# The first attention's value projection in two blocks side by side, its index weights in four, with a PSUM bank of their own

## The chip, the core and the metric

The kernel runs on one NeuronCore of a Trainium2 chip. The metric is the device time of one launch in microseconds (us), as the median of three runs; the kernel before takes 1764.91 us (1761.79 to 1765.24). The core has a matrix engine (TensorE, "PE" in the rows; its weight loads are listed apart as "PEld"), a vector engine (DVE), a scalar engine (ACT), GpSimd (POOL), and SyncE (SP), which issues most of the DMAs. Each works through its own list of instructions in order and waits for the others at semaphores.

## The reference

Two model blocks follow each other over 1024 tokens of width 1024. The first normalises its input, scales and shifts it by a vector made from a condition, projects it (`w_in`), and sends the parts through a state space mixer and through an attention in which each query keeps the 256 best keys by an index score. The second is a block with dilated window attention and a chunked scan. What the change touches is the projection of the first attention's values `v` (64 wide) and of the index weights `wi` (8 wide):

```python
h = rms_norm(x, norm_g) * (1 + scale[:, None]) + shift[:, None]
proj = h @ w_in
xa, za, q, k, v, zb, qi, ki, wi, ga, gb = jnp.split(proj, IN_SPLITS, axis=-1)
...
s = jax.nn.relu(jnp.einsum('bqhd,bkd->bqhk', qib.astype(f32), k_idx32)) * IDX_SCALE
score = jnp.einsum('bqh,bqhk->bqk', wb.astype(f32), s)
_, sel = lax.top_k(score, top_k)
```

Here `qib`, `k_idx32` and `wb` are `qi`, `ki` and `wi`; 64 + 8 = 72 output features are at stake.

## The kernel before

The projections are a list of *units* (`unit_plan`, L230). A unit fills one PSUM bank with an output of 128 features by 512 tokens: PE multiplies in eight steps `k`, one for each 128 input features, accumulating in the bank; then ACT copies the bank out (`evac`, L1957) and counts `s_free`. `unit_bank` (L322) says which bank a unit has, and a unit waits until the last unit of its bank is copied out.

The first ten units (`FIRST_ORDER`) work in fp32 on `h_whole`, the transposed, normalised input. Of these `("small", 0)` and `("small", 1)` (units 0 and 4 of the list) make `v` and `wi` together, with 72 weight columns, for the first and the second half of the tokens: eight matmuls each, 72 output rows by 512 tokens. In the trace one fp32 matmul is two weight loads and two matmul records; in this kernel these two units therefore are 16 + 16 records of "128*72 128x512 f32" at L1416. `("small", 2)` and `("small", 3)` make the keys and index keys with full 128 columns. `("small", 4)` and `("small", 5)` transpose what units 0 and 4 left in `vwT` (L1367), and wait for the copying out of unit 4.

The order on PE is written out by hand (L1652 to L1679): ten warming products (L1653); the transposes of the input's first half (L1626); the products for scale and shift (`mod_products`, L1639, whose weights are loaded by four DMAs, and `mod_turned`, L1647); steps 0 to 3 of unit 0 (`unit(0, 0)`); the other scale and shift products; steps 0 to 3 of unit 1; steps 4 to 7 of unit 0 and of unit 1; unit 2; the transposes of the second half; unit 3; units 4 to 9. Each step `k` of unit 0 waits until DVE (even `k`) or ACT (odd `k`) has scaled and shifted its part of `h_whole`. The transposes of the input use banks 2 to 7 in the first half and banks 4 to 7 in the second (`input_bank`). After unit 9 the index scores (L1694) begin, in banks 2 to 7.

ACT works in this order around the place: squares of the input for the norm, scaling of half of `h_whole` (L2147), more squares, an `Exp`, the copying out of units 0 and 1, some `Exp` and `Sin` for the state space part, the eight scaled copies of the second half's transposes (L2177), then units 2, 3, 4 and so on. `evac` of unit 0 or 4 is one instruction of 72 partitions by 512 (L1964).

A fact of the listing that is needed later: a row such as "128*64 128x128 f32" says that the matmul uses 128 rows and 64 columns of the array (a *form* of the array, here called the 64-column form) and moves 128x128 elements through it. Other stages of this kernel use narrow forms already: L1445, L1860 and L1865 (64 columns), L1716 (32 columns), L1393 (16 columns), L1526 (64 rows by 32 columns).

Of the kernel before, what the change touches and what calls it, by code (L numbers as in the profile page):

```python
# [10 lines left out]
ACT = mybir.ActivationFunctionType  # L11
AX_X = mybir.AxisListType.X

P = 128
# [199 lines left out]


SMALL_COLS = 216


NORM_PARTS = ((0, 2), (2, 4), (4, 8))
# [102 lines left out]
def unit_bank(u):  # L322
    if UNITS[u][0] in ("gb1", "gate0", "gate1"):
        return 0
    if UNITS[u][0] in ("q", "zs0", "zs1") or UNITS[u] in LATER_ORDER:
        return u % 2
    if UNITS[u][0] == "xa":
        return UNITS[u][1] % WIDE_BANKS
    if UNITS[u][0] == "pair0":
        return UNITS[u][1] % 2  # L330
    if UNITS[u][0][:3] == "woA":
        return OUT_BANKS[(u - FIRST["woA0"]) % len(OUT_BANKS)]
    return (u + 2) % WIDE_BANKS
# [13 lines left out]
def layer_kernel(nc, x, mods, first_weights, loads, groups, params, consts, rows, alibi, out, x2_dram, gates_dram, q_dram,  # L347
                 sums_dram, res_dram):
    ctx = ExitStack()
    with ctx:  # L350
# [933 lines left out]
        def _(pe):  # L1284
            mm = nc.tensor.matmul

            def operands(name, i):

                whole = name in WHOLE
                w = W[:, LOADS.index(name) % 2, :] if name in LOADS else None

                def weights(steps, k, c0, n):
                    if name == "small":
                        return small_w[:, k, c0:c0 + n]
                    if name in PLANAR:
                        return planes(chunks(MADE_AT[name][k], 1))
                    if steps == KD and name in MADE_AT:
                        v = chunks(MADE_AT[name][k], 1)[:, c0:c0 + n]  # L1300
                        return v if whole else parts(v)
                    v = w.rearrange("p (k n) -> p k n", k=steps)[:, k, c0:c0 + n]
                    return v if whole else parts(v)

                def acts(tile, k, t0, n):
                    if whole:
                        return h_whole[k][:, t0:t0 + n]
                    return h_parts(k, t0, n) if tile is hT else parts(tile[:, k, t0:t0 + n])

                half = (i % 2) * 512  # L1310
                full = slice(0, 512)
                if name[:4] == "gate":
                    return 1, [(full, lambda k: ones, lambda k: gate[:, 512 * int(name[4]):512 * int(name[4]) + 512])]
                if name == "small" and i < 2:
                    return KD, [(full, lambda k: weights(KD, k, P, 72), lambda k: acts(hT, k, half, 512))]
                if name == "small":
                    return KD, [(full, lambda k: weights(KD, k, 0, P), lambda k: acts(hT, k, half, 512))]
                if name == "qi" and i % 2 == 0:
                    return KD, [(slice(TOPK, 512), lambda k: weights(KD, k, (i // 2) * P, P),
                                 lambda k: acts(hT, k, TOPK, 512 - TOPK))]  # L1320
                if name == "glu":
                    c0 = (i % 2) * 512 + (i // 4) * P
                    h0 = ((i // 2) % 2) * 512
                    return 4, [(full, lambda k: weights(4, k, c0, P), lambda k: planes(yaT[:, k, :])[:, h0:h0 + 512, :])]
                if name == "ao":
                    return 4, [(full, lambda k: weights(4, k, (i // 2) * P, P), lambda k: planes(zaT[:, k, half:half + 512]))]
                if name == "bo":
                    h0 = (i // 8) * 512
                    return 4, [(full, lambda k: weights(4, k, (i % 8) * P, P), lambda k: block_planes(ybT[:, k, h0:h0 + 512]))]
                if name in ("out0", "out1"):  # L1330
                    src = mT
                    return KD, [(full, lambda k: acts(src, k, i * P, P), lambda k: weights(KD, k, 0, 512))]
                if name[:4] == "pair":
                    what, h = PAIR_UNITS[i]
                    c0 = P * "qkvz".index(what)
                    return KD, [(full, lambda k: weights(KD, k, c0, P), lambda k: acts(hT, k, h * 512, 512))]
                if name[:2] == "wo":
                    src = mixS if name[2] == "S" else mixA
                    return KD, [(full, lambda k: acts(src, k, i * P, P), lambda k: weights(KD, k, 0, 512))]

                return KD, [(full, lambda k: weights(KD, k, (i // 2) * P, P), lambda k: acts(hT, k, half, 512))]

            def unit(u, share=None):
# [43 lines left out]
                if name == "dt":  # L1387
# [7 lines left out]
                                          stop=(k == KD - 1 and (a, b) == PRODUCTS[-1]), skip_group_check=True)  # L1395
                    last.then_inc(s_unit, 1)
                    return
                rows_ = slice(0, 72 if name == "small" and i < 2 else P)
                steps, pieces = operands(name, i)
                some = range(steps)  # L1400
                if share is not None and len(pieces) == 1:
# [4 lines left out]
                for (cols, lhs, rhs), span in spans:  # L1406

                    for k in span:
                        if (name, i) == ("small", 0):
                            pe.wait_ge(s_hta if k % 2 else s_htv, k // 2 + 1)  # L1410
                        if (name, i) == ("xbc0", 1):
                            pe.wait_ge(s_hlow, KD + KD + k + 1)
                        left, right = lhs(k), rhs(k)
                        o = ps[rows_, unit_bank(u), cols]
                        if whole:
                            last = mm(o, left, right, start=(k == 0), stop=(k == steps - 1))  # L1416
                            continue
                        if len(right.shape) == 4:
                            o = o.rearrange("p (b t) -> p b t", t=P)
                        for a, b in PRODUCTS:  # L1420
                            moving = right[:, :, b] if len(right.shape) == 3 else right[:, :, :, b]
                            last = mm(o, left[:, :, a], moving, start=(k == 0 and (a, b) == PRODUCTS[0]),  # L1422
                                      stop=(k == steps - 1 and (a, b) == PRODUCTS[-1]))
# [192 lines left out]
            def turn_input(n):  # L1616

                k, half = turned(n)
                if k == 0:
                    pe.wait_ge(s_xn, 4 * half + 4)  # L1620
                if 6 <= n < KD:
                    pe.wait_ge(s_xt_read, n - 5)
                elif n >= KD:
                    pe.wait_ge(s_xt_read, max(n - 3, KD))
                for j in range(4):
                    last = nc.tensor.transpose(ps[:, input_bank(n), j * P:(j + 1) * P],  # L1626
                                               XR0[:, 4 * half + j, k * P:(k + 1) * P], ident)
                last.then_inc(s_xt, 1)
# [319 lines left out]
        def _(act):  # L1948
# [8 lines left out]
            def evac(u):  # L1957
# [3 lines left out]
                bank = ps[:, unit_bank(u), :]  # L1961
                half = slice((i % 2) * 512, (i % 2) * 512 + 512)
                if name == "small" and i < 2:
                    last = A(vwT[0:72, half], bank[0:72], ACT.Copy)  # L1964
                elif name == "small" and i < 4:

                    for tile, rows_ in ((kT1, slice(0, 64)), (kiT, slice(64, 128))):
# [1341 lines left out]
```

## Time and profile before

| | |
|---|---|
| median of three runs | 1764.91 us (1761.79 to 1765.24) |
| profiled execution, its time | 1763.56 us |
| profiled execution, span from first to last instruction | 1761.8 us |
| PE busy | 1724.0 us, 98% of the span |
| PE's waits over 0.1 us, before 81 us | eight, 6.4 us together; of it 0.17 us after 38 us |
| DVE, POOL, ACT busy | 67%, 50%, 46% |

In a row of the timeline the first number is the start in us from the span's start, the second the length, then engine, line, operation, what is written and read, the form, and how many records were merged; in brackets the idle time just before and what ended it. A matmul's record begins when its data start to move and lasts longer than its place in the stream: records of one engine overlap, so the price of a matmul in a dense stream is the distance between starts. A weight load can overlap the matmul before it. The table of waits and the groups say who waits for whom; the rows themselves stand below.

### The profile page before, as it was taken

The numbers are of one execution on the slowest core, as the hardware profiler recorded it, in microseconds if no ns is written. First come the engines' busy times: TensorE is split into PE (matmuls) and PEld (weight loads), VectorE is DVE, ScalarE is ACT, GpSimd is POOL, SyncE is SP. The second block draws the span as 40 slices with busy tenths as digits, with TensorE's granted clock in tenths as the row PEclk, the third lists the DMA queues.
The fourth block names the chain that finished last, engine by engine and source line by source line (L and its number), as shares of the span: only waits on it lengthen the run. The fifth ranks groups of instructions, "written<-read, shape, count | busy, mean of one in ns | idle before, by whom it ended". The sixth has DMA issues, their size and how long they took to land.

```text
span 1761.8 us, 30529 instructions
## 1 busy us (share of the span) xinstructions
PE 1724.0 (98%) x11938; PEld 891.6 (51%) x11938; DVE 1182.8 (67%) x2237; ACT 813.6 (46%) x1628; POOL 887.1 (50%) x805
## 2 busy tenths in 40 slices
PE   8999999999999999999999999999999999999998
PEld 5534455555444466544544455544455555555543
DVE  5759889999999788532345677966155565654637
ACT  4523554443322577412332468733255555555710
POOL 0511443652671222696911177969556555772750
PEclk9999999999999999999999999999999999999999
DMA  9010111102321112212512346512211111111512
GB/s 396 32 54 36 55 49 62 71 37 102 161 96 48 73 67 103 120 48 96 201 63 94 111 145 198 186 54 96 68 40 53 56 42 51 35 52 55 216 58 96
DMA packets 53375, 161.87 MB, mean 92 GB/s; under 512 B 7056, under 2 KB 21776, under 8 KB 49008
## 3 DMA queue, kind: packets, MB, share of 16 engines
q1 hardware_dynamic: 49008, 136.36, 21.8%
q0 software_dynamic: 4224, 23.56, 3.4%
q8 instruction: 95, 1.56, 0.4%
q14 instruction: 48, 0.39, 0.1%
HBM read 129.35 MB, written 27.39 MB: 89 GB/s over the span
## 4 chain that ended last, share of the span: by engine, by line
PE 67%; DVE 20%; ACT 4%; POOL 3%; DMA 3%; issue 2%; SPq 0%; DVEq 0%; ACTq 0%; POOLq 0%
PE ps L1422 28%; PE ps L1901 15%; DVE small L2684 6%; PE ps L1416 4%; DVE arena L2437 4%; PE ps L1762 2%; PE ps L1445 2%; PE ps L1486 2%; PE ps L1544 2%; PE ps L1920 2%; DMA hT<-in_mods 2%; PE ps L1518 1%; PE ps L1694 1%; PE ps L1459 1%; PE ps L1526 1%
## 5 line engine op out<-in xcount | busy, mean ns | idle before, releaser
L1422 PE MATMUL ps<-hT,W 128*128 128x512 bf16 x2424 | 536.5, 380 | 4.1 <-ACT arena L2004 3.2
L1422 PEld LDWEIGHTS ps<-hT,W 128*128 128x128 bf16 x2424 | 235.7, 98 | 288.3 <-issue 10.2
L989 POOL TENSOR_TENSOR W<-W 128x512 bf16<-128x512 f32 x133 | 153.9, 1193 | 248.5 <-DMA W<-in_loads 181.8
L1422 PE MATMUL ps<-W,arena 128*128 128x512 bf16 x936 | 208.2, 380 | 0.0
L2111 ACT ACTIVATE arena<-arena,small 128x128 f32<-128x128 f32 (+9 forms) x192 | 123.1, 642 | 139.0 <-DVE small L2514 119.6
L1422 PEld LDWEIGHTS ps<-W,arena 128*128 128x128 bf16 x936 | 91.2, 97 | 112.0
L2684 DVE TENSOR_SCALAR_CACHE_REDUCE small<-arena,small 128x640 bf16<-128x640 f32 (+1 forms) x124 | 126.5, 1077 | 1.1
L974 POOL TENSOR_TENSOR arena<-arena 128x512 f32<-128x512 f32 (+1 forms) x62 | 104.8, 1690 | 43.9 <-DMA arena<-gates_scratch 20.1
L1422 PE MATMUL ps<-arena,W 128*128 128x512 bf16 x576 | 125.0, 379 | 0.6 <-POOL arena L1050 0.6
L2120 ACT ACTIVATE arena<-arena,small 128x128 f32<-128x128 f32 (+9 forms) x192 | 113.9, 644 | 18.6 <-DVE small L2472 18.6
L1901 PE MATMUL ps<-arena,W 128*128 128x512 bf16 x492 | 112.9, 379 | 0.0
L2490 DVE TENSOR_TENSOR arena<-ps,arena 128x384 bf16<-128x384 f32 (+2 forms) x128 | 57.0, 466 | 64.4 <-ACT arena L2088 41.1
L3148 DVE TENSOR_TENSOR arena<-ps,arena 128x512 f32<-128x512 f32 x70 | 50.9, 728 | 63.3 <-PE ps L1901 63.3
L1422 PEld LDWEIGHTS ps<-arena,W 128*128 128x128 bf16 x576 | 56.2, 98 | 69.4 <-POOL arena L1050 1.1
L1901 PE MATMUL ps<-hT,W 128*128 128x512 bf16 x384 | 88.4, 380 | 0.0
L2437 DVE TENSOR_TENSOR arena<-arena,small 128x512 f32<-128x512 f32 (+2 forms) x74 | 82.7, 1143 | 0.7
L2009 ACT ACTIVATE arena<-ps 128x512 f32<-128x512 f32 x48 | 28.3, 596 | 118.5 <-PE ps L1422 70.5
L1109 POOL COPY arena<-small 128x128 bf16<-128x128 bf16 x32 | 17.2, 538 | 130.3 <-DVE small L2437 130.1
L1213 POOL TENSOR_TENSOR W<-W 128x512 bf16<-128x512 f32 x73 | 79.8, 1120 | 1.1
L1901 PEld LDWEIGHTS ps<-arena,W 128*128 128x128 bf16 x492 | 47.8, 98 | 49.7 <-issue 0.7
L2514 DVE CUSTOM_DVE_ANT_0 arena<-ps,arena 128x256 f32<-128x256 f32 (+7 forms) x128 | 61.9, 516 | 11.1 <-PE ps L1526 9.3
L2447 DVE COPY arena<-ps 128x512 f32<-128x512 f32 (+3 forms) x96 | 49.0, 552 | 26.2 <-PE ps L1486 25.9
(392 smaller groups left out, 3223.6 us busy)
## 6 DMA issues: line engine op xcount, KB each, us to landing
W<-in_loads SPq DMA_DIRECT2D x20, 2048.0 KB, 7.9
arena<-sums_scratch SPq DMA_DIRECT2D x30, 512.0 KB, 4.7
W<-in_groups SPq DMA_DIRECT2D x56, 256.0 KB, 3.9
W<-in_loads SPq DMA_DIRECT2D x5, 1792.0 KB, 7.2
gates_scratch<-arena SPq DMA_DIRECT2D x32, 256.0 KB, 2.0
arena<-gates_scratch POOLq DMA_DIRECT2D x2, 4096.0 KB, 13.6
W<-in_mods SPq DMA_DIRECT2D x2, 2048.0 KB, 17.1
hT<-in_mods SPq DMA_DIRECT2D x2, 2048.0 KB, 21.3
```

The costliest lines, as they stand in the source:

```text
L974: return nc.gpsimd.tensor_tensor(o, a, b, ALU.mult)
L989: last = nc.gpsimd.tensor_tensor(low(v), v, high(v), ALU.subtract)
L1213: nc.gpsimd.tensor_tensor(low(v[name]), v[name], high(v[name]), ALU.subtract).then_inc(s_block, 1)
L1416: last = mm(o, left, right, start=(k == 0), stop=(k == steps - 1))
L1422: last = mm(o, left[:, :, a], moving, start=(k == 0 and (a, b) == PRODUCTS[0]), stop=(k == steps - 1 and (a, b) == PRODUCTS[-1]))
L1901: last = mm(ps[:, bank, :], w[:, :, a], moved(right, k, b), start=(first and k == 0 and (a, b) == PRODUCTS[0]), stop=(k == 3 and (a, b) == ...
L2111: A(t, t, ACT.Exp, bias=mneg4[:, (n % 2) * 2 + x:(n % 2) * 2 + x + 1], scale=-1.0, accum_out=den[:, (n % 2) * 2 + x:(n % 2) * 2 + x + 1]). ...
L2120: A(t, t, ACT.Copy, scale=rden[:, (n % 2) * 2 + x:(n % 2) * 2 + x + 1]).then_inc(sems["scaled"], 1)
L2437: return V.tensor_tensor(o, a, b, ALU.mult)
L2490: last = V.tensor_tensor(to[:, LOW, cols], ps[:, 6 + x, cols], to[:, HIGH, cols], ALU.subtract)
L2514: V.tensor_tensor_reduce(at2["rows"][n % 2][x][:, 0:window(i)], ps[:, 2 + x, 0:window(i)], bias_of(items[n], x), -ATTN_SCALE, BIG, ALU.add ...
L2684: V.tensor_scalar(junk[b], sc_at(i), levels[b], None, ALU.is_ge, ALU.add, accum_out=count4[:, b:b + 1]).then_inc(s_v, 1)
```

## The change

For units 0 and 4, each step `k` is no longer one matmul of 72 columns by 512 tokens but six: two for `v` (64 columns, 256 tokens each, written to partitions 0 to 63 and 64 to 127 of the unit's bank), and four for `wi` (8 columns, 128 tokens each, written to partitions 0, 32, 64 and 96 of bank 4, `INDEX_BANK`). ACT copies the unit out with six instructions in place of one. As bank 4 is also used by the transposes of the input's second half, the first of these now waits for unit 0's copy too. Everything else is as it was; the lines behind the place are numbered 13 to 19 higher.

```diff
+INDEX_BANK = 4
...
-                if name == "small" and i < 2:
-                    return KD, [(full, lambda k: weights(KD, k, P, 72), lambda k: acts(hT, k, half, 512))]
...
-                rows_ = slice(0, 72 if name == "small" and i < 2 else P)
+                if name == "small" and i < 2:
+
+                    span = range(KD) if share is None else range(KD // 2) if share == 0 else range(KD // 2, KD)
+                    for k in span:
+                        if i == 0:
+                            pe.wait_ge(s_hta if k % 2 else s_htv, k // 2 + 1)
+                        for c in range(2):
+                            t0 = 512 * i + 256 * c
+                            mm(ps[DH * c:DH * c + DH, unit_bank(u), 0:256], small_w[:, k, P:P + DH], h_whole[k][:, t0:t0 + 256],
+                               start=(k == 0), stop=(k == KD - 1), skip_group_check=True)
+                        for r in range(4):
+                            t0 = 512 * i + P * r
+                            last = mm(ps[32 * r:32 * r + 8, INDEX_BANK, 0:P], small_w[:, k, P + DH:P + DH + 8],
+                                      h_whole[k][:, t0:t0 + P], start=(k == 0), stop=(k == KD - 1), skip_group_check=True)
+                    if share != 0:
+                        last.then_inc(s_unit, 1)
+                    return
...
@@ turn_input
                 if k == 0:
                     pe.wait_ge(s_xn, 4 * half + 4)
+                    if half:
+                        pe.wait_ge(s_free, UNITS.index(("small", 0)) + 1)
...
@@ evac
                 if name == "small" and i < 2:
-                    last = A(vwT[0:72, half], bank[0:72], ACT.Copy)
+                    for c in range(2):
+                        A(vwT[0:DH, 512 * i + 256 * c:512 * i + 256 * c + 256], bank[DH * c:DH * c + DH, 0:256], ACT.Copy)
+                    for r in range(4):
+                        last = A(vwT[DH:DH + 8, 512 * i + P * r:512 * i + P * r + P], ps[32 * r:32 * r + 8, INDEX_BANK, 0:P],
+                                 ACT.Copy)
```

The program for PE from steps 4 to 7 of unit 0 (the 72x512 row) to the first product of unit 2, in the kernel before; a name such as `ps<-arena` is what is written and read, and a count is of matmuls:

```order
L1416 MATMUL ps<-arena 128x512 x4
L1416 MATMUL ps<-arena 72x512 x4
L1416 MATMUL ps<-arena 128x512 x4
L1416 MATMUL ps<-arena,W 128x256 x8
L1626 MATMUL ps<-ck,arena 128x128 x32
```

And the same place after the change, where L1405 is the value block and L1409 the index weights:

```order
L1429 MATMUL ps<-arena 128x512 x4
L1405 MATMUL ps<-arena 64x256 x2
L1409 MATMUL ps<-arena 8x128 x4
L1405 MATMUL ps<-arena 64x256 x2
L1409 MATMUL ps<-arena 8x128 x4
L1405 MATMUL ps<-arena 64x256 x2
L1409 MATMUL ps<-arena 8x128 x4
L1405 MATMUL ps<-arena 64x256 x2
L1409 MATMUL ps<-arena 8x128 x4
L1429 MATMUL ps<-arena 128x512 x4
L1429 MATMUL ps<-arena,W 128x256 x8
L1641 MATMUL ps<-ck,arena 128x128 x32
```

Four matmuls have become 24, in two shapes that alternate; nothing around them has moved. Unit 4 reads the same way with eight steps, and unit 0's first four steps too.

On ACT, the copying out of units 0 and 1 before the change:

```order
L2166 ACTIVATE small<-pk 128x16
L1964 ACTIVATE arena<-ps 72x512
L1969 ACTIVATE arena<-ps 64x512 x4
L2170 ACTIVATE small<-small 128x16
L2171 ACTIVATE small<-small 128x16
```

And after it:

```order
L2185 ACTIVATE small<-pk 128x16
L1980 ACTIVATE arena<-ps 64x256 x2
L1982 ACTIVATE arena<-ps 8x128 x4
L1988 ACTIVATE arena<-ps 64x512 x4
L2189 ACTIVATE small<-small 128x16
L2190 ACTIVATE small<-small 128x16
```

One copy has become six, in the same place; it is so for unit 4 too.

## Rows read from the trace of the kernel before

**Rows 1.** Busy time of the engines, from the page.

```profile
PE 1724.0 (98%) x11938; PEld 891.6 (51%) x11938; DVE 1182.8 (67%) x2237; ACT 813.6 (46%) x1628; POOL 887.1 (50%) x805
```

**Rows 2.** Timeline of PE, the first 82 us.

```profile
25.65 3.63 PE L1416 MATMUL ps<-arena 128*72 128x512 f32 x8 [1.26 <-DVE arena L2575]
...
32.23 2.05 PE L1639 MATMUL ps<-arena,hT 128*128 128x128 f32 x16 [1.17 <-DMA hT<-in_mods]
...
37.63 10.46 PE L1416 MATMUL ps<-arena 128*128 128x512 f32 x24
47.93 3.62 PE L1416 MATMUL ps<-arena,W 128*128 128x256 f32 x16
51.39 1.91 PE L1626 MATMUL ps<-ck,arena 128*128 128x128 f32 x16
53.47 2.66 PE L1626 MATMUL ps<-ck,arena 128*128 128x128 f32 x16 [0.17 <-ACT arena L2177]
...
59.42 13.90 PE L1416 MATMUL ps<-arena 128*72 128x512 f32 x32
73.16 0.67 PE L1367 MATMUL ps<-ck,arena 72*128 72x72 f32 x8
```

**Rows 3.** Timeline of ACT, 20 to 90 us.

```profile
44.88 0.57 ACT L1964 ACTIVATE arena<-ps 72x512 f32<-72x512 f32 x1
48.13 2.40 ACT L1969 ACTIVATE arena<-ps 64x512 f32<-64x512 f32 x4 [2.68 <-PE ps L1416]
...
66.49 0.59 ACT L1964 ACTIVATE arena<-ps 72x512 f32<-72x512 f32 x1 [0.28 <-PE ps L1416]
73.36 2.40 ACT L1969 ACTIVATE arena<-ps 64x512 f32<-64x512 f32 x4 [6.27 <-PE ps L1416]
```

**Rows 4.** Timeline of PE around 1034 us: two lines in the 64-column form.

```profile
1028.64 5.34 PE L1422 MATMUL ps<-hT,W 128*128 128x512 bf16 x24
1033.92 0.44 PE L1860 MATMUL ps<-arena 128*64 128x128 f32 x4
1034.18 0.40 PE L1865 MATMUL ps<-arena 128*64 128x128 f32 x4
...
1035.49 0.40 PE L1865 MATMUL ps<-arena 128*64 128x128 f32 x4
1035.82 1.12 PE L1868 MATMUL ps<-arena 128*128 128x512 f32 x2
```

**Rows 5.** Timeline of PE at 209 us: the 32-column form; second, from 209.4 only.

```profile
209.35 2.02 PE L1716 MATMUL ps<-arena 128*32 128x128 f32 x64
211.30 1.90 PE L1422 MATMUL ps<-hT,W 128*128 128x512 bf16 x8
...
209.14 0.27 PE L1711 MATMUL ps<-ck,arena 128*128 128x128 f32 x1
```

**Rows 6.** Instructions of one line each: duration in ns, min/median/max.

```profile
L1860 PE MATMUL ps<-arena x256: 272/273/323, 1026.4 to 1151.1; 128*64 128x128 f32 x128
L1716 PE MATMUL ps<-arena x256: 272/273/297, 209.3 to 398.4; 128*32 128x128 f32 x128
L1393 PE MATMUL ps<-hT,small x192: 218/219/225, 909.0 to 911.7; 128*16 128x128 bf16 x192
```

**Rows 7.** Timeline of PE at 1288 us: from one narrow form to another.

```profile
1287.61 0.50 PE L1518 MATMUL ps<-arena 64*128 64x256 bf16 x6
1288.04 0.53 PE L1526 MATMUL ps<-arena 64*32 64x128 bf16 x24
```

**Rows 8.** ACT groups kept apart by shape: busy, mean ns.

```profile
L2019 ACT ACTIVATE small<-ps 16x128 f32<-16x128 f32 x8 | 2.1, 267 | 0.2 <-PE ps L1393 0.2
L1975 ACT ACTIVATE arena<-ps 128x256 f32<-128x256 f32 x4 | 1.6, 400 | 3.9 <-PE ps L1416 3.9
```

**Rows 9.** Timeline of PE at 339 us, and the granted clock there.

```profile
338.75 7.04 PE L1422 MATMUL ps<-hT,W 128*128 128x512 bf16 x24 [3.18 <-ACT arena L2004]
...
339.60:343.00 3.40, 3.40 (x9) 0.50 0.60 223
```

**Rows 10.** The chain that ended last, 165 to 240 us.

```profile
176.68 2.71 PE ps L1422 x12
179.41 0.61 ACT arena L2013
...
180.40 8.90 DMA W<-in_loads
...
189.43 10.22 POOL W L989 x7
```

More of the change, by code:

```diff
@@ L1408, in unit @@
                     for k in span:
-                        if (name, i) == ("small", 0):
-                            pe.wait_ge(s_hta if k % 2 else s_htv, k // 2 + 1)
                         if (name, i) == ("xbc0", 1):
@@ L1413, in unit @@
                         left, right = lhs(k), rhs(k)
-                        o = ps[rows_, unit_bank(u), cols]
+                        o = ps[:, unit_bank(u), cols]
                         if whole:
```

## Prediction

> **What bounds the kernel now.** I read the page's busy line first: PE works 98% of the span, 1724.0 of 1761.8 us [rows 1]. So a microsecond put into PE's stream or taken out of it is a microsecond of the kernel, unless PE waits soon afterwards for something that does not move with it. Next the timeline of PE for the first 82 us [rows 2]. Before 38 us PE still waits: 1.26 us for the scaled input at 25.65, and 1.17 us at 32.23 for a weight DMA of the modulation, which does not depend on PE. From 37.63 to 73.16 the stream is dense but for 0.17 us at 53.47, a wait for ACT. ACT in turn had waited for PE (2.68 us before 48.13, for unit 1's end) and worked on from there [rows 3], so this wait moves along with PE. The change falls on three pieces: steps 0 to 3 of unit 0 (the 25.65 row), ahead of the DMA wait; steps 4 to 7 of unit 0, inside the x24 row at 37.63; and the eight steps of unit 4, the first half of the x32 row at 59.42. The last two, 12 steps together, are on the path.
>
> **What a step costs now.** The x32 row from 59.42 to 73.16 is 13.74 us for 16 fp32 matmuls, 0.859 us each, or 0.429 a record [rows 2]. The 72-column matmuls of unit 4 and the 128-column ones of unit 5 share that row and that price: narrowing the weights alone buys nothing.
>
> **What a step costs afterwards.** The new step has two kinds of work.
>
> Values: two matmuls of 64 columns by 256 tokens. A 256-column record costs 0.216 us: (51.39 − 47.93)/16 [rows 2]. Two matmuls have four records, on two lanes (column halves of the array). Do the lanes run side by side? L1860 and L1865 are in just this form and dtype: four records of 128 columns each start 1035.49 − 1034.18 = 0.218 us after the four before them (1035.49 − 1034.18 = 1.31 us for six such groups), 0.055 a record [rows 4]. On one lane a 128-column record is worth half of a 256-column one, 0.108. So two lanes do run at once: 2 x 0.216 = 0.432 us for the values.
>
> Index weights: four matmuls of 8 columns by 128 tokens, eight records on four lanes. L1716 has that with 32 columns: 64 records from 209.35 to 211.30, 0.030 a record with all edges in it [rows 5], a quarter of 0.108 and a little. So 2 x 0.109 = 0.218 us.
>
> That is 0.650 us against 0.859, a gain of 0.209 a step. But the step also changes the form of the array twice, and this has a price in every place where the trace shows it. From the last L1711 record (209.14, a 128-column record worth 0.108) to the first L1716 one (209.35) there are 0.10 us too many [rows 5]. From L1422 (24 records of 0.216 from 1028.64 end at 1033.82) to L1860 at 1033.92: 0.10. Out of it again, from 1035.49 plus 0.218 to 1035.82: 0.11 [rows 4]. And between two narrow forms, L1518 to L1526: six bf16 records of 256 on two lanes are 3 x 0.107 = 0.32, the distance is 0.43: 0.11 [rows 7]. Between L1860 and L1865, which share a form, nothing is added. I take 0.10 a change. Besides, the first records after a change begin with their weights not yet loaded: the longest L1860 is 50 ns over the median, the longest L1716 24, and L1393 with 16 columns 6 [rows 6]. For 64 columns I take 0.05, for 8 columns 0.01.
>
> The Trainium skill says this plainly: in "TensorEngine Tiling (Array Packing)", Tiling Modes, Key Properties, changing the tiling mode, not just the tile, drains the engine, while different tiles load and multiply in parallel. The trace agrees with both halves: 0.10 us a change of form, and 0.055 us a record within one. By the page's speed-up alone, without its drain, the sum would be a gain of 12 x 0.209 = 2.5 us; with it the sum is as follows.
>
> A step after: 0.432 + 0.218 + 0.05 + 0.01 + 2 x 0.10 = 0.91 us, 0.05 more than now. For 12 steps on the path that is 0.6 us. Each run of steps also has one more change of form than two a step (in from the 128-column form, out to it): 2 x 0.10 = 0.2. Sum on the path: **+0.8 us**. The bounds: with a change at 0.09 and the loads hidden, 12 x (0.65 + 0.18 − 0.859) + 0.18 = −0.2; with 0.11 and 0.074 for the loads, 12 x (0.65 + 0.22 + 0.074 − 0.859) + 0.22 = +1.2. I take the value in the middle since most rows say 0.10.
>
> **What I cost at nothing.** Steps 0 to 3 of unit 0 get 4 x 0.05 + 0.1 = 0.3 us longer, and L1639 behind them waits 1.17 us for a DMA anyway [rows 2]; without that cover 0.3 us would be added. ACT's copying out of unit 0 goes from 0.57 us to two copies of 256 columns at 0.40 and four of 128 at 0.27 [rows 8]: 1.87, so 1.3 us more. ACT had 2.68 us of waiting before the next unit and 6.27 us after unit 4's copy [rows 3]; neither is used up, and L1969 still starts when PE ends its unit. Uncovered it would be 1.3 us for each. The new wait of the second half's first transpose is for a copy that ends near 47 us, and the transpose starts at 51.39 [rows 2]; behind it on PE stand the 32 transposes and all that follows, so it would hurt if it bit, but 4 us are between. Unit 4's copy must be ready for the transposes at 73.16; it would end near 69. DVE, POOL and SP have no instruction added or moved. PE gets 16 x 20 more records and as many loads; L1716 passes 64 of each in 1.95 us [rows 5], closer together than the new steps need (24 of both in 0.91 us), so the feeding of the queue is no bound.
>
> The profiled execution took 1763.56 us, its span 1761.8, 1.8 outside it; plus 0.8 is 1764.4 for its like. It lies 1.35 below the median of the runs. On the median: 1764.9 + 0.8 = **1765.7 us**.
>
> **The rivals.**
>
> *Strict order of starts (slower).* The records of one lane stand next to each other in the program: both passes of the first value block, then both of the second. If a record could not start before all ahead of it had, the second lane's first pass would wait for the first lane's second. The values would take 3 x 0.216 and the index weights 5 x 0.109: 1.193 us, with 0.26 for changes and loads 1.45 a step, 0.59 over now; 12 of these and 0.2 give +7.3 us, 1772.2. "TensorE: Matmul & The Clock Gate", Part 3, The mechanism, in the Trainium skill says this of matmuls: strict order in start and end, no reordering. The trace speaks against it: L1716 issues four records to one lane, then four to the next, and under that order its 16 lots would take three places each, 16 x 3 x 0.108 = 5.2 us; they take 1.95 [rows 5]. The reordering would have to fail for the new shapes, where each lane's record is twice as long. If the lanes don't overlap at all, a step is 4 x 0.216 + 8 x 0.109 + 0.26 = 2.0 us, and +13.9 gives 1778.8. The point from which this decides is a step of 1.15 us.
>
> *No price between the two column forms (faster).* No row shows 128 rows by 64 columns next to 128 by 32. If the array changes between these freely, a step is 0.66, 12 x 0.20 = 2.4 us are won and four edges cost 0.4: −2.0, 1762.9. For it: both are narrow forms over all 128 rows. Against it: [rows 7], where also only the columns change, and pay 0.11.
>
> *Something further on answers.* At 338.75 PE comes from 3.18 us of waiting, and from 339.60 to 343.00 the granted clock is 0.50, the lower level of 1.2 GHz; the 24 records there take 7.04 us where the same 24 take 5.34 [rows 4, 9], so the stretch costs 1.7 us. If a shift makes that wait shorter the clock may stay up; if it makes another wait longer it may fall once more. Either sign, 1.7 us, more with the waits themselves: 1763.2 to 1768, and rarely past 0.2%.
>
> *Hidden anyway.* The chain that ended last leaves PE at 179 us: ACT copies a unit out, SP then loads weights for 8.90 us, and POOL splits them [rows 10]; only later does it come back to PE. It starts from a unit that PE has made, so it should move along with PE; if what PE waits for at 338.75 [rows 9] hangs on something else, the 0.8 is swallowed: 1764.9.
>
> **How the numbers follow.** 0.2% is 3.5 us, about what a measurement of this kernel can tell from no change. Chances: the forecast, with the swallowed case in its range of 1763.5 to 1767.5, 0.64; no price between the forms 0.11; strict order 0.07 and no overlap 0.03; an answer further on 0.15. Faster by more than 0.2% needs the second and the clock together or an answer that I don't see: 0.08. Slower: 0.10 for the two cases of order, and 0.04 for an answer further on: 0.14. Within 0.2%: 0.78. The range, 1761.5 to 1770, leaves out the order cases and the far ends of the others.
>
> **What would show it.** In the new timeline L1405 and L1409 alternate; the starts of two L1405 rows should be 0.91 us apart, each L1409 group starting 0.58 after its L1405 group; unit 4 should take 7.4 us from its first record to unit 5's first, where it takes 6.9 now. The transposes of `vwT` (73.16 now) should start near 74.0, L1639's DMA wait shrink to about 0.9, L1969 keep an idle time before it. I am wrong in the price of a change if the distance is 0.65 to 0.75, in the order if it is 1.4, in the cover if a wait for `s_free` shows before the second half's transposes.

## The result, and the profile after

The changed kernel took 1773.97 us (median of 4 runs, 1770.89 to 1774.32) against 1764.56 for the kernel before (4 runs, 1761.79 to 1765.24): a ratio of 1.0054, 95% interval 1.0042 to 1.0066. It is slower, by 9.4 us, above the forecast (1765.7) and above the end of the range (1770). The profiled execution took 1773.98 us, its span 1772.2: 10.4 us more than the 1761.8 of before.

At the place itself the forecast held. This is the timeline of PE after the change, over unit 0's first piece, the DMA wait, and unit 4 (it answers to [rows 2]):

```profile
25.55 0.65 PE L1405 MATMUL ps<-arena 128*64 128x256 f32 x4 [1.26 <-DVE arena L2594]
26.13 0.41 PE L1409 MATMUL ps<-arena 128*8 128x128 f32 x8
26.46 0.65 PE L1405 MATMUL ps<-arena 128*64 128x256 f32 x4
...
32.08 2.05 PE L1654 MATMUL ps<-arena,hT 128*128 128x128 f32 x16 [0.81 <-DMA hT<-in_mods]
...
59.80 0.65 PE L1405 MATMUL ps<-arena 128*64 128x256 f32 x4
60.38 0.41 PE L1409 MATMUL ps<-arena 128*8 128x128 f32 x8
60.72 0.65 PE L1405 MATMUL ps<-arena 128*64 128x256 f32 x4
...
67.14 7.13 PE L1429 MATMUL ps<-arena 128*128 128x512 f32 x16
74.11 0.67 PE L1366 MATMUL ps<-ck,arena 72*128 72x72 f32 x8
```

A step begins 0.917 us after the one before it ((67.14 − 59.80)/8; forecast 0.91), the index weights 0.58 behind their values (forecast 0.58), unit 4 takes 7.34 us (forecast 7.4), and the transposes of `vwT` start at 74.11, 0.95 later than at 73.16 (forecast 0.8). The DMA wait at 32.08 shrank from 1.17 to 0.81 us, as it should; but it also ended 0.15 us earlier than at 32.23, on its own account, so what the change put on the path is 0.95 + 0.15 = 1.10 us, inside the bounds of the forecast (−0.2 to +1.2). ACT's longer copying is hidden (it answers to [rows 3]):

```profile
67.28 0.77 ACT L1980 ACTIVATE arena<-ps 64x256 f32<-64x256 f32 x2 [0.79 <-PE ps L1409]
68.06 1.11 ACT L1982 ACTIVATE arena<-ps 8x128 f32<-8x128 f32 x4
74.31 2.40 ACT L1988 ACTIVATE arena<-ps 64x512 f32<-64x512 f32 x4 [5.15 <-PE ps L1429]
```

Its six copies end at 69.17, and 5.15 us of waiting are left. So a net 0.95 of the 10.4 us is there at 74 us. The other 9.4 come up where the change has no instruction. I compared the start of the same instruction in both timelines, stage by stage: the shift is 1.0 us until 486, 2.3 behind it, 2.7 from 862 to 911, 7.7 at 919, 10.7 at 935, and 10.4 at the end. Here is the largest part; first the timeline of PE before, around 909 us:

```profile
909.02 2.86 PE L1393 MATMUL ps<-hT,small 128*16 128x128 bf16 x192
913.18 0.64 PE L1383 MATMUL ps<-ck,small 16*128 16x16 f32 x8 [1.31 <-ACT small L2019]
913.75 10.53 PE L1422 MATMUL ps<-hT,W 128*128 128x512 bf16 x48
```

And after, the same three pieces of work:

```profile
911.71 2.80 PE L1392 MATMUL ps<-hT,small 128*16 128x128 bf16 x188
919.51 0.28 PE L1392 MATMUL ps<-hT,small 128*16 128x128 bf16 x4 [5.00 <-issue]
921.11 1.00 PE L1382 MATMUL ps<-ck,small 16*128 16x16 f32 x8 [1.31 <-ACT small L2038]
922.05 12.92 PE L1435 MATMUL ps<-hT,W 128*128 128x512 bf16 x48
```

The run of 192 short products (the units named `dt`, 0 and 1: 16 columns, starts 14 ns apart) stops after 188 for 5.00 us, released by nothing that the profile shows ("issue"). Behind it the same work is slower (8 products by 0.36 us, the next 48, the wide products whose results the convolution takes and which I call the conv products, by 2.4), and the table of stretches says why (stretch and its length in us, PE's busy time and its matmuls, granted clock, DMA share, GB/s):

```profile
909.00:913.00 4.00, 4.00 (x105) 1.00 0.11 22
913.00:918.00 5.00, 1.51 (x110) 0.87 0.97 299
918.00:923.00 5.00, 2.17 (x15) 0.50 0.59 215
923.00:928.00 5.00, 5.00 (x16) 0.61 0.00 0
```

After PE had stood still the granted clock was 0.50, the level of 1.2 GHz, until about 927; before the change it was 1.00 over all of 909 to 928. The stop is 5.0 us and the clock 3.0 (10.7 − 7.7) of the 10.4. The small rest, 0.4 us on the way to 862 and 0.3 given back at the end, I can't assign: on another chip 25 executions of the kernel before ran from 1761.64 to 1768.26 us, and each kernel has one profiled execution.

A smaller piece is at 486 us. The timelines of POOL, before and after:

```profile
468.28 4.04 POOL L989 TENSOR_TENSOR W<-W 128x512 bf16<-128x512 f32 x4 [3.13 <-DMA W<-in_loads]
```

```profile
470.61 4.04 POOL L990 TENSOR_TENSOR W<-W 128x512 bf16<-128x512 f32 x4 [4.42 <-DMA W<-in_loads]
```

and of PE after, where before there was no such wait:

```profile
488.23 4.06 PE L1435 MATMUL ps<-arena,W 128*128 128x512 bf16 x18 [1.32 <-ACT arena L2013]
```

The weight load that POOL waits for lands 1.3 us later than its issue explains (18.0 us from issue to landing, 16.8 before), so POOL is later for ACT, and ACT for PE: +1.25.

What brings in a stop with no releaser? Such a stop alone says little: PE has one of 1.0 us near 274 us in every kernel here, with the change and without. The page's table of DMA queues has a queue of instructions; before and after:

```profile
q8 instruction: 95, 1.56, 0.4%
```

```profile
q8 instruction: 96, 1.57, 0.4%
```

Packets and MB: 16 KB each, and the third number is their share of the DMA engines' time. PE has 24,348 instructions in the trace before (11,938 matmuls, as many weight loads, and 472 others), 24,668 after. Divided by the packets that is 256 and 257: I take a packet to be a block of 256 PE instructions. (The kernels below bear this out: 95 packets up to 24,412 PE instructions, 96 from 24,540 to 24,732, 97 from 24,796 on.) The change adds 160 matmuls and 160 loads, 320 instructions: everything behind 67 us lies 64 further on than a whole block. In what follows I call the number of PE instructions that a kernel has more than before, modulo 256, its **offset**: 64 for the change.

### The profile page after: what moved, and what is told of

Read it like the earlier page. It is cut to its first block, busy times and chain, and to the rows that moved or that the text cites. A ratio compares the mean times of both kernels' runs of the same rounds, so it can differ in the third digit from the quotient of the medians.

```text
span 1772.2 us, 30859 instructions
## 1 busy us (share of the span) xinstructions
PE 1728.6 (98%) x12098; PEld 892.8 (50%) x12098; DVE 1189.8 (67%) x2237; ACT 816.6 (46%) x1638; POOL 885.1 (50%) x805
## 4 chain that ended last, share of the span: by engine, by line
PE 67%; DVE 20%; ACT 4%; POOL 3%; issue 3%; DMA 3%; SPq 0%; DVEq 0%; ACTq 0%; POOLq 0%
PE ps L1435 28%; PE ps L1916 15%; DVE small L2703 6%; DVE arena L2456 4%; PE ps L1429 3%; PE ps L1777 2%; PE ps L1458 2%; PE ps L1499 2%; PE ps L1557 2%; PE ps L1935 2%; DMA hT<-in_mods 2%; PE ps L1531 1%; PE ps L1709 1%; PE ps L1472 1%; PE ps L1539 1%
```

## The experiments

The theory: PE's instructions come in blocks of 256, and the dense run at 909 us (384 instructions that start within 2.64 us) uses them faster than blocks arrive; whether it runs dry depends on where in a block it starts, so on the offset, and not on what the change does. The rival: the new form of the step, or the 1 us of shift, meets something at 909 us in another way.

The tool for it is a number of tiny spare products, 8 columns by 8 elements, 4 PE instructions and about 0.02 us each, in places where PE waits anyway (behind the warm-up, before the wait for the first modulation, before the last modulation products):

```diff
+            def spare_products(n, bank, source):
+                for q in range(n):
+                    r = q % 4
+                    mm(ps[32 * r:32 * r + 8, bank, 0:8], source[:, 0:8], source[:, 0:8], start=True, stop=True,
+                       skip_group_check=True)
...
+            spare_products(16, 0, still)
...
+            spare_products(16, 7, ones)
             pe.wait_ge(s_mod, 1)
...
+            spare_products(16, 7, ones)
             mod_products(MOD_ORDER[3])
```

The kernel before was run again with each group of experiments, on the same chip (medians of 1764.13, 1763.94 and 1763.50 us), and each ratio is against those runs; between groups compare the ratios.

**1. The change with 48 spare products (offset 0).**

> The changed kernel with 48 tiny fp32 matmuls (8 columns by 8, results unused) spread over three places before 33 us where PE waits anyway; each makes two loads and two matmul records, so 192 more records stand ahead of everything later. Theory A (instruction loading): the 5.00 us stop of PE at 914.5 us in the changed kernel comes where a fast run of narrow matmuls (L1392, 384 records in 2.8 us) uses up its instructions before the next 16 KB block of them, 256 instructions of 64 bytes, has been loaded; which part of a block the run falls on is set by how many instructions stand before it. The change added 320, that is 64 past a whole block; 192 more make 512, two whole blocks, so the run falls where it did before the change. The stop and the half clock behind it go: about 5.0 + 2.7 us back, 1766.5 us, 0.1% over before. Rival B (time): the stop comes because the whole program is 1 to 2.7 us later and meets a load or another queue at the wrong moment; the padding hardly moves the time, so the stop stays and the time is 1774.

Measured: 1766.19 us, ratio 1.0008 (0.9999 to 1.0017). POOL's wait near 468 is 3.17 us, and the run has its 192 products in one row, without a stop:

```profile
910.52 2.86 PE L1392 MATMUL ps<-hT,small 128*16 128x128 bf16 x192
```

7.8 us are gone, with the change itself untouched.

**2. The kernel before with 16 spare products (offset 64).** Only the spare products in the middle place.

> The kernel before, with 16 tiny fp32 matmuls (64 records) where PE waits 1.26 us at 25.65 us for the scaled input; nothing else is changed and nothing on the path gets longer. Theory A: 64 records shift the fast run at L1393 to the same part of a block as in the changed kernel, so the 5 us stop and the half clock appear without the change: 1764.6 + 5.0 + 2.7 = 1772.3 us, +0.44%. Rival B: time is not moved by more than 0.1 us at any later place, so no stop: 1764.6.

Measured: 1771.29 us, ratio 1.0044 (1.0027 to 1.0060). The kernel before, with nothing of the change in it, gets the change's stop at the same product:

```profile
911.59 2.80 PE L1393 MATMUL ps<-hT,small 128*16 128x128 bf16 x188
919.02 0.29 PE L1393 MATMUL ps<-hT,small 128*16 128x128 bf16 x4 [4.62 <-issue]
920.60 1.00 PE L1383 MATMUL ps<-ck,small 16*128 16x16 f32 x8 [1.30 <-ACT small L2027]
921.53 12.18 PE L1422 MATMUL ps<-hT,W 128*128 128x512 bf16 x48
```

The half clock is there too (0.51 over 918 to 923 us), and POOL's 4.42 us and PE's 1.31 us at 488 as well. The shift of the early stages is −0.24 us here, +1.0 in the change, and the new form is absent: the form of the step isn't needed for the stop. By 909 us the shift is 2.6 us here as in the change, 1.1 of it from a longer stay at 339 us, so this run by itself doesn't rule out the time of arrival; experiment 5 does.

**3. The kernel before with 48 spare products (offset 192).**

> The kernel before with the 48 tiny matmuls (192 records) of after_pad192, the control for their own cost. Theory A: by the position of the loads in the trace, the run falls on a part of a block where it ends before instructions run out: no stop, 1764.6 to 1765.0. If any padding costs time by itself, this shows it. Rival B: no stop either, 1764.6 to 1765.0; only a third theory, that any added instruction makes the stop, expects 1772.

Measured: 1765.41 us, ratio 1.0004 (0.9995 to 1.0014), no stop at 910 (it has another, see experiment 4): 128 more instructions than in experiment 2 put the time back. The spare products themselves cost nothing that I can measure.

**4. Where in a block does it decide?** The change with 16 spare products (offset 128), and the kernel before with 8 (offset 32).

> The changed kernel with 16 tiny matmuls at 25 us: 64 more records, 384 in all against the kernel before, 128 past a whole block of 256. Theory A in numbers: in the changed kernel the load of the next block starts 5.4 us after the fast run began (917.12 to 911.71) and PE goes on 2.4 us after that start; PE had used the last block up 375 records into the run. With 64 more it uses it up after 311 records, 2.1 us into the run, while the load is asked for 64 records sooner, 11 records ahead of the run, 1.2 us before it at the slow pace there. So it goes on about 6.1 us after the run's start: a stop of about 3.9 us, after 311 +- 10 records, in place of 5.0 after 376. If the stop were only a matter of 64 past a block, or of the time, it would be absent, or at the same record with the same length.

> The kernel before with 8 tiny matmuls (32 records) at 25 us. Theory A: the last loaded block ends 407 records after the run's start, 23 after its end (the 384 of L1393, the 16 of L1383, then L1422). The load is asked for 32 records later than in before_pad64, 0.2 us: PE could go on 8.0 us after the run's start and has reached the spot after 5.1 us, since the wait for ACT (1.3 us) lies between: a stop of about 2.5 to 3 us in the first products of L1422, and some half clock: 1767 to 1769 us. Rival: no stop outside the fast run: 1764.6.

Measured: 1770.06 us, ratio 1.0038 (1.0024 to 1.0053), and 1771.47, ratio 1.0036 (1.0021 to 1.0051). The timeline of PE, offset 128:

```profile
910.80 2.36 PE L1392 MATMUL ps<-hT,small 128*16 128x128 bf16 x156
914.21 0.68 PE L1392 MATMUL ps<-hT,small 128*16 128x128 bf16 x36 [1.05 <-issue]
```

and offset 32:

```profile
910.38 2.86 PE L1393 MATMUL ps<-hT,small 128*16 128x128 bf16 x192
914.54 0.64 PE L1383 MATMUL ps<-ck,small 16*128 16x16 f32 x8 [1.30 <-ACT small L2027]
915.34 0.59 PE L1422 MATMUL ps<-hT,W 128*128 128x512 bf16 x2 [0.16 <-issue]
919.45 3.14 PE L1422 MATMUL ps<-hT,W 128*128 128x512 bf16 x7 [3.51 <-issue]
```

(In the traces of experiment 4, and in those of `grouped` with offsets 64 and 192, some matmul records are missing, for example 11,952 matmuls for 12,130 loads with offset 128. Each row of 47 conv products is one of 48 with a record lost, and a gap of 0.16 us at its start is that record.)

The place of the stop is the block's end: 64 instructions more ahead of the run move it 64 instructions forward, from product 188 to 156 (376 to 312 instructions in the run; I expected 311), and 32 fewer move it behind the run, 408 instructions after its start, into the conv products. The lengths came out otherwise than I expected: 1.05 us where I said 3.9, and 3.51 where I said 2.5 to 3. And by the ratios after_pad64 is 5 us over after_pad192 (1.0038 for 1.0008), of which the rows at 910 explain 1.1 and those at 488 about 1.2. The profiled executions are only 1.7 us apart (spans of 1767.1 and 1765.4): that of after_pad64 was the fastest of its four, that of after_pad192 the second slowest of its ten. The rest is in executions that no profile shows; it stays open.

The two kernels with offset 192 have a stop of their own that no other kernel has, 0.64 us before 863.39 in before_pad192 and 0.70 before 861.51 in grouped_pad128, released by nothing either. The last block's packet started 9 us ahead of it, so it isn't like the others; I did not follow it up.

What sets the length? The start of the instruction block in the trace of packets gives one half of the answer. PE went on 2.2 to 2.5 us after it in each of the five stops so far (917.12 to 919.51 in the change, 916.82 to 919.02, 911.87 to 914.21, 916.95 to 919.45, and 914.26 to 916.67 in experiment 5). So the length hangs on when the block's packet starts. In four of the five this was 5.2 to 6.6 us after the first product of the run; with offset 128, where the stop was short, 1.1 us, at 911.87, just ahead of the first data packet at 911.88. And 0.1 us after the first product SP issues something, in before and in the change:

```profile
909.12 0.33 SPq L804 DMA_DIRECT2D W<-in_loads  x1
```

```profile
911.81 0.33 SPq L805 DMA_DIRECT2D W<-in_loads  x1
```

This is the weight load of `xbc2`, 1792 KB, which waits for the unit ahead of `dt` and takes 8.2 us; its first data packet starts 1.1 us after the run's first product. Experiment 6 is about it.

**5. Can the change win at another order?** `grouped` makes all value products of a piece first, then all index products: three changes of form a piece instead of two a step and one. Offset 64 without spare products; I ran it so, and with 48 (offset 0) and 32 (offset 192).

```diff
+                    for k in span:
                         for r in range(4):
                             t0 = 512 * i + P * r
                             last = mm(ps[32 * r:32 * r + 8, INDEX_BANK, 0:P], ...
```

> The grouped order without padding, so 320 records more than before, as in the changed kernel. Theory A: the 5.0 us stop and the half clock are back: 1762.4 + 7.5 = 1769.9 us, 4 us under the changed kernel, whose place costs 2.6 us more. If grouping had removed the stop (a theory in which the stop comes from what the place does), 1762.4.

> The changed kernel with its matmuls in another order: in each of the three pieces (steps 0 to 3 of unit 0, 4 to 7 of unit 0, all of unit 4) all value blocks first, then all index weights; so each piece has three changes of form and not two a step and one. With the padding of after_pad192. Form theory: a piece of n steps takes n x 0.65 + 0.30 + 0.06, 2.96 us for 4 steps (3.44 before the change, 3.67 after) and 5.56 for 8 (6.87 before, 7.35 after): 1.8 us less than before at the place, and with theory A no stop at 914 us: 1764.6 - 1.8 = 1762.8. If the changes of form cost nothing by themselves (the order of starts or the loads take the time), the pieces stay at 3.6 and 7.3 us and the time is near after_pad192's. Rival B on the stop: it may be there or not, the time then 1770.

> The grouped order with 32 tiny matmuls in two places instead of 48 in three: 448 records more than before, 192 past a whole block. Theory A: the run ends before its instructions do, as in before_pad192: no stop, 1762.4 like grouped_pad192, 0.1% under the kernel before. A stop of 4 us or more would speak against the reckoning with blocks of 256.

Measured: 1772.72 us with offset 64, ratio 1.0050 (1.0032 to 1.0069, 2 runs); 1762.36 with offset 0, ratio 0.9991 (0.9981 to 1.0000); 1763.05 with offset 192, ratio 0.9995 (0.9986 to 1.0004). Unit 4 in the one with offset 0 (L1410 is the line of the index weights here):

```profile
59.01 3.67 PE L1405 MATMUL ps<-arena 128*64 128x256 f32 x32
62.61 1.93 PE L1410 MATMUL ps<-arena 128*8 128x128 f32 x64
64.47 7.13 PE L1430 MATMUL ps<-arena 128*128 128x512 f32 x16
71.44 0.67 PE L1366 MATMUL ps<-ck,arena 72*128 72x72 f32 x8
```

5.46 us for the unit, 1.9 less than with forms that alternate and 1.4 less than before; the `vwT` transposes start 1.7 us earlier than before. That is the gain that two lanes and four lanes side by side have to give, and the price of a form change, together with the first weight loads behind it, shown by its absence: 14 changes and 7 sets of first loads fewer in unit 4, for 1.88 us (by the forecast's prices 14 x 0.10 + 7 x 0.06 = 1.82). But the same kernel at offset 64 has the stop in full, and loses more than it won:

```profile
908.86 2.80 PE L1392 MATMUL ps<-hT,small 128*16 128x128 bf16 x188
916.67 0.29 PE L1392 MATMUL ps<-hT,small 128*16 128x128 bf16 x4 [5.01 <-issue]
```

Here the run starts 0.16 us earlier than in the kernel before, which has no stop: being late isn't what brings it. The 1772.72 us, from two executions, are 2.8 over the 1769.9 that I expected; that sum left out the wait at 486 us, 1.4 us in this trace, and the rest stays open.

**6. The weight load at the run's start.** In four kernels the load of `xbc2` waits for the end of `dt` instead of for the unit ahead of it; no other line is changed, and the offsets stay. SP issues in order, so the two DMAs behind this load, 256 KB into `ck` and 512 KB to `gates_scratch`, move with it: the experiment takes all three away from the run.

```diff
+                elif LOADS[n] == "xbc2":
+                    sp.wait_ge(s_unit, FIRST["dt"] + 3)
                 elif n >= 2:
                     sp.wait_ge(s_unit, unit_end(LOADS[n - 2]))
```

> The kernel before with 16 tiny products (64 more PE records), in which it stopped for 4.62 us after 188 of the 192 products of dt and took 1771.29 us; now the weight load of xbc2 (1792 KB and 256 KB), which SP issued 0.1 us after the first of these products, waits for the end of dt (3 units, about 4 us later). Theory (the 16 KB block of PE's instructions is held back by the packets of this weight load): the block arrives before the run is through, the stop goes to 0 to 1 us and the half clock behind it (2.7 us) with it: 1771.3 - 4.6 - 2.7 = 1764.0 us, at most 1765. Rival (the block is asked for late, or takes as long, by PE's own loading alone): the stop stays at 4 to 5 us and the time at 1771 us. In between (half of each), the stop is 2 to 3 us and the clock falls all the same: 1768 to 1769 us.

> The grouped order of the change without spare products (stop of 5.01 us, 1772.7 us), with the weight load of xbc2 put behind dt. Theory: no stop and no half clock, 1772.7 - 5.0 - 2.7 = 1765.0 us, with the 1.2 us at 488 us left in it. Rival (PE's own loading): 1772 to 1773 us.

> The changed kernel as it is (stop of 5.00 us, 1774.0 us), with the weight load of xbc2 put behind dt. Theory: no stop and no half clock, 1774.0 - 5.0 - 2.7 = 1766.3 us. Rival (PE's own loading): 1773 to 1774 us.

> The kernel before, which has no stop there, with the weight load of xbc2 put behind dt: what the move costs or brings by itself. Both theories: the load has 40 us of slack (POOL waits for W at 965 us for units, not for it), so nothing: 1763.5 to 1765 us. If it is later than 1766 us, the weight load was needed earlier than its reader shows.

Measured:

| kernel | offset | us | ratio (95%) | without the move |
|---|---|---|---|---|
| before_pad64_late | 64 | 1767.51 | 1.0020 (1.0011 to 1.0029) | 1771.29 |
| grouped_late | 64 | 1766.17 | 1.0013 (1.0004 to 1.0023) | 1772.72 |
| after_late | 64 | 1769.36 | 1.0034 (1.0022 to 1.0045) | 1773.97 |
| before_late | 0 | 1763.77 | 0.9997 (0.9987 to 1.0006) | – |

The stop is still after product 188 in all three with offset 64, but short. after_late:

```profile
910.70 2.80 PE L1394 MATMUL ps<-hT,small 128*16 128x128 bf16 x188
914.81 0.23 PE L1394 MATMUL ps<-hT,small 128*16 128x128 bf16 x4 [1.31 <-issue]
916.35 1.00 PE L1384 MATMUL ps<-ck,small 16*128 16x16 f32 x8 [1.30 <-ACT small L2040]
917.29 13.37 PE L1437 MATMUL ps<-hT,W 128*128 128x512 bf16 x48
917.38 0.33 SPq L807 DMA_DIRECT2D W<-in_loads  x1
```

before_pad64_late:

```profile
913.80 0.23 PE L1395 MATMUL ps<-hT,small 128*16 128x128 bf16 x4 [1.13 <-issue]
915.34 0.64 PE L1385 MATMUL ps<-ck,small 16*128 16x16 f32 x8 [1.30 <-ACT small L2029]
915.91 12.22 PE L1424 MATMUL ps<-hT,W 128*128 128x512 bf16 x48
```

In grouped_late the stop is 0.96 us. The packets show why. In the changed kernel, the DMA queues of the stretch 911 to 917 us have only the data (queue, kind: packets, MB, share), and the instruction block comes in the next microsecond:

```profile
q1 hardware_dynamic: 91, 1.30, 68.5%
```

```profile
q1 hardware_dynamic: 18, 0.26, 110.8%
q8 instruction: 1, 0.02, 5.8%
```

In after_late the stretch 911 to 913 us has nothing but the block:

```profile
q8 instruction: 1, 0.02, 3.4%
```

It started 1.62 us after the first product there, 5.41 after it in the change: the data held it back by 3.8 us, and the stop is 3.7 us shorter without them. Up to the block's start only 1.30 MB had been taken up in the change, less than the 1792 KB of the first load, so it is this load that the block stood behind, as far as the traces tell; I did not move the loads one by one. The mechanism of the theory stands, but not the expected times. The stop did not go to 0 to 1 us, it is 1.0 to 1.3, since PE goes on 2.4 us after the block's start, and this comes 1.4 to 1.6 us into a run that is through with the block ahead after 2.8. And the half clock stays: the 48 conv products take 13.37 us in after_late, 12.22 in before_pad64_late and 11.93 in grouped_late, against 10.53 before. So the times are over the expected ones: by 3.5 us in before_pad64_late, 3.1 in after_late and 1.2 in grouped_late.

## Why the prediction was wrong

**What was right.** The price of the new step (0.917 for 0.91), with the form changes of 0.10 us in it; the sum at the place (+1.10 on the path for +0.8, within the bounds of −0.2 to +1.2); the cover of the first piece by the DMA wait; ACT's longer copies at no cost; and the two rivals on order and on free changes of form: the step would have been 1.4 or 0.66. That the measured 1774 us lies near the 1772.2 of the rival with strict order is chance: the step of 0.917 us excludes it.

**The step that failed** is the last one of "What I cost at nothing": "PE gets 16 x 20 more records and as many loads ... so the feeding of the queue is no bound". The comparison was of rates at the place, and there it holds. What it left out is that the 320 extra instructions stay in the count for the rest of the program. They move every block border behind them by 64 instructions, and at the dense run, where PE uses up a block in less time than the next takes to come, that decides whether the border falls on a block that is there. Measured in its place: 5.0 us of stop and 3.0 us of lower clock behind it, and 1.25 us at 486 with the same offset. Most of the parts could be read before the run: 24,348 instructions in 95 packets of 16 KB, a run of 384 instructions that start 6.9 ns apart, a whole block in 1.8 us, and a load of 1792 KB that starts with it. The 2.2 to 2.5 us from a packet's start to PE going on could not: only a kernel that stops there shows them. (The sentence also counts double: 24 for 4 in each of 16 steps is 320 with the loads in it, not 320 of each.)

Here the Trainium skill, in "Runtime: NRT & Kernel Launch", Instruction fetch mechanics, would have misled as well as helped: it gives the 16 KiB blocks of 256 instructions, which the packets confirm, and then says that fetching is hidden because the engine issues more slowly than blocks arrive. The trace disagrees: 5.00 us of it were not hidden.

**The rival nearest to it**, "something further on answers", had the right place in the argument and the wrong size. I worked it out from the one half-clock stretch that the trace before showed, 1.7 us; the answer was 9.4 us: 5.0 of stop, 3.0 of clock, 1.25 at 486 and 0.4 on the way to 862, less 0.3 given back at the end. The half clock that I feared at 338.75 stayed as it was (7.01 us for the 24 records, 7.04 before); another was added behind the stop.

**What is shown and what is only argued.** Shown by runs: the stop depends on the number of PE instructions ahead (offset 0 and 192 have none at this place, 32, 64 and 128 do, in kernels with the change and without it); and its length on the DMAs that start with it, the 1792 KB load first of them. The +1.25 us at 486 goes with the same offsets: POOL's wait for the weight load is 4.1 to 4.5 us in the runs with offset 32, 64 and 128, and 3.1 to 3.3 in those with 0 and 192. In the first the block's packet starts 2.6 to 13 us before that load ends, in the others at most 0.7 us before its end, or after it. And the load takes 17.8 to 18.1 us from issue to landing in the first, 16.7 to 16.9 in the others. That the packet delays the load's last ones is a guess from this; I moved nothing there to test it. The 0.4 us before 862 and the rest between after_pad64 and after_pad192 stay open too.

Without the stop the change costs 1.4 us or nothing (1.0008, interval 0.9999 to 1.0017), which agrees with the forecast. The best version, grouped with 48 spare products, is 1.8 us below the kernel before it on the same chip, with an interval that touches 1 (0.9981 to 1.0000): not a gain that I would claim.

## What to carry to other kernels

Count the instructions that a change adds to an engine, not only their time: each moves the block borders of all that follows, and a change can lose several microseconds hundreds of microseconds behind its place. Where a trace shows the same instruction packets as here, look before a prediction for stretches in which an engine uses 256 instructions in less than the 2.2 to 2.5 us measured here (the dense run takes 1.8), and for large data loads that start together with them; there the number of instructions ahead decides. And before a kernel version is called slower, shift it by some spare instructions in a waiting place (for the change 192 did it, and 64 did not): a loss that goes away with them is not the change's own.

## What the runs showed of the hardware

- PE's instructions come in packets of 16 KB, 256 instructions each (95 packets for 24,348). From the start of a packet to the first instruction that needed it PE took 2.2 to 2.5 us, in eight stops.
- Behind a 1792 KB weight load issued 0.1 us after the run's start, the packet started 5.2 to 6.6 us after the run's start; without that load 1.4 to 2.4 us. The exception is offset 128: its packet started 1.1 us after the run's start, ahead of the load's first data. At offset 64 the stop grew from 1.0–1.3 to 4.6–5.0 us.
- A stop of 1.13 us with the wait of 1.30 us behind it was followed by a granted clock of 0.80 over 918 to 923 us; and one of 0.96 us (grouped_late) by 0.66 over 913 to 918. With offset 128 a stop of 1.05 us, with 36 products in place of 4 between it and that wait, left the clock at 1.00 and the next 48 conv products at full speed (10.95 us from the row of 8 ahead of them to the row behind, 10.94 before). So the length of the stop alone does not decide; what does, these runs don't say.
- Alternating a 64-column and an 8-column form costs more than running side by side gives: 0.917 us a step, against 0.68 (5.46/8) with the same matmuls grouped and 0.859 for the one wide matmul.
